# Spreading the adaLN modulation pairs of a two-block transformer kernel over more stages

## The reference

```python
def first_block(x, ...):
    ...
    h = rmsnorm(x, norm_ffn_pre[l])
    u = causal_depthwise_conv(h @ w_ffn_up[l], ffn_conv_w[l], ffn_conv_b[l])
    u_gate, u_val = jnp.split(u, 2, axis=-1)
    y = (jax.nn.gelu(u_gate, approximate=True) * u_val) @ w_ffn_down[l]
    return x + rmsnorm(y, norm_ffn_post[l])

def second_block(x, c, ctx, c_ctx, w_mod, b_mod, ...):
    for l in range(2):
        m_lat = (silu(c) @ w_mod[l] + b_mod[l]).reshape(9, 1024)
        m_ctx = (silu(c_ctx) @ w_mod[l] + b_mod[l]).reshape(9, 1024)
        x_lat = ffn_sublayer(x_lat, m_lat, 0, ...)      # rms_norm, scale and shift by m, swiglu, gate by m
        x_ctx = ffn_sublayer(x_ctx, m_ctx, 0, ...)
        p = modulate(rms_norm(x, ...), m, 1) @ w_in[l]   # q, k, v, fourier, gates
        ...                                              # attention, fourier mixing, gated merge
        x = ffn_sublayer(x, m, 2, ...)
```

## Time and profile before

| what | value |
|---|---|
| time, median of 3 runs | 2647.0 us (2645.97 to 2647.9) |
| profiled execution | 2647.9 us, its span 2646.1 us |
| TensorE busy | 2569.3 us, 97% of the span |
| VectorE busy | 1399.3 us, 53% |
| GpSimd busy | 1307.9 us, 49% |
| ScalarE busy | 1072.8 us, 41% |
| loaded from HBM | 363.19 MB, 138 GB/s over the span |

### The profile page before, as it was taken

How to read it: one execution, slowest core, us unless ns; L and a number is a source line. 1 busy time by engine, 2 the same in 40 slices (tenths; PEclk the granted TensorE clock), 3 DMA queues, 4 the chain that set the end, 5 groups by cost and what they waited for, 6 DMA issues and landing times.

```text
span 2646.1 us, 42582 instructions
## 1 busy us (share of the span) xinstructions
PE 2569.3 (97%) x14948; PEld 2232.8 (84%) x14948; DVE 1399.3 (53%) x3175; ACT 1072.8 (41%) x1934; POOL 1307.9 (49%) x654
## 2 busy tenths in 40 slices
PE   7999999999999999999999999999999999999998
PEld 7968999997788888877788888888888888889998
DVE  3656845358885420365476555665554443645221
ACT  4445457542223342266534222342222342565443
POOL 4515868754444443243344443444444453456885
PEclk8999989999999999999999999999999999999999
DMA  6714745635555432121234444544443452324563
GB/s 199 231 56 154 235 137 186 189 104 189 190 190 150 136 111 95 33 80 48 82 110 143 143 143 129 166 134 143 143 139 118 140 185 77 104 96 144 172 191 114
DMA packets 414006, 365.87 MB, mean 138 GB/s; under 512 B 7484, under 2 KB 412558, under 8 KB 413888
## 3 DMA queue, kind: packets, MB, share of 16 engines
q1 hardware_dynamic: 411448, 359.14, 43.0%
q10 hardware_dynamic: 2440, 5.16, 0.6%
HBM read 363.19 MB, written 1.08 MB: 138 GB/s over the span
## 4 chain that ended last, share of the span: by engine, by line
PE 74%; issue 11%; POOL 10%; DVE 3%; ACT 2%; DMA 0%; POOLq 0%; SPq 0%; ACTq 0%; DVEq 0%
PE bank L1978 61%; POOL w_lo L787 10%; PE bank L2498 2%; PE bank L2064 1%; PE bank L2538 1%; PE bank L2065 1%; PE bank L2069 1%; PE bank L2442 1%; PE bank L2310 1%; PE bank L2306 1%; DVE stat L1884 1%; ACT w_hi L837 1%; PE bank L2434 1%; PE bank L2190 1%; PE bank L2524 0%
## 5 line engine op out<-in xcount | busy, mean ns | idle before, releaser
L787 POOL TENSOR_TENSOR w_lo<-raw,w_hi 128x1024 fp32r<-128x1024 f32 (+3 forms) x558 | 1212.1, 2186 | 1153.1 <-ACT w_hi L837 1152.7
L837 ACT ACTIVATE w_hi<-raw 128x1024 fp32r<-128x1024 f32 (+3 forms) x558 | 533.0, 975 | 1014.4 <-PE bank L1978 703.8
L1978 PE MATMUL bank<-u_hi,w_hi 128*128 128x512 f32 (+1 forms) x2456 | 835.2, 340 | 8.3 <-POOL w_lo L787 4.0
L1978 PE MATMUL bank<-u_hi,w_lo 128*128 128x512 f32 (+1 forms) x2456 | 829.0, 338 | 0.0
L1978 PE MATMUL bank<-u_lo,w_hi 128*128 128x512 f32 (+1 forms) x2456 | 828.9, 338 | 0.0
L1978 PEld LDWEIGHTS bank<-u_hi,w_hi 128*128 128x128 f32 x2456 | 467.2, 190 | 81.9 <-issue 29.5
L1978 PEld LDWEIGHTS bank<-u_hi,w_lo 128*128 128x128 f32 x2456 | 467.4, 190 | 49.4
L1978 PEld LDWEIGHTS bank<-u_lo,w_hi 128*128 128x128 f32 x2456 | 467.6, 190 | 47.5
L1493 DVE SCALAR_TENSOR_TENSOR bank<-mod_raw,cond,bank 128x256 f32<-128x256 f32 x1008 | 401.4, 485 | 0.1
L1978 PE MATMUL bank<-hid_hi,w_hi 128*128 128x512 f32 (+1 forms) x880 | 305.6, 347 | 0.1
L1978 PE MATMUL bank<-hid_hi,w_lo 128*128 128x512 f32 (+1 forms) x880 | 305.0, 347 | 0.0
(11 more groups left out here) (272 smaller groups left out, 3424.2 us busy)
## 6 DMA issues: line engine op xcount, KB each, us to landing
raw<-in_ffn_w_in SPq DMA_DIRECT2D x88, 1024.0 KB, 5.1
mod_raw<-in_w_mod SPq DMA_DIRECT2D x144, 512.0 KB, 4.5
raw<-in_w_in SPq DMA_DIRECT2D x67, 1024.0 KB, 5.1
raw<-in_ffn_w_out SPq DMA_DIRECT2D x56, 704.0 KB, 4.7
raw<-in_w_ffn_up SPq DMA_DIRECT2D x22, 1024.0 KB, 5.1
raw<-in_w_attn_out SPq DMA_DIRECT2D x8, 1024.0 KB, 5.2
raw<-in_w_o SPq DMA_DIRECT2D x8, 1024.0 KB, 5.2
raw<-in_w_ffn_down SPq DMA_DIRECT2D x8, 704.0 KB, 4.6
```

The lines of the kernel that those rows point to most:

```text
L787: pool.tensor_tensor(st.half(t, w_lo[slot]), st.half(t, block), st.half(t, w_hi[slot]).bitcast(f32), ALU.subtract).then_inc(lo_ready, 1)
L837: act.activation(st.half(t, w_hi[(st.first + c) % 2]), st.half(t, raw_of(st, n)), ACT.Copy).then_inc(hi_ready, 1)
L1978: ins = pe.matmul(dst, s, v, start=first and n == 0, stop=final and n == 2)
```

## The change

Ten of the twenty pairs that `up_00` did are taken out of it (`mod=2` becomes `mod=1` over its bodies 1 to 10). They go to: `down1` (bodies 0, 1 and 2, one each), `down_00` (seven where there were four), `q_0` (one, in its second body), `k_0` (two) and `f_0` (one). The total, 36 for layer 0, stays. In `down1` DVE does the pair after the two tiles of the body, not between them. On ACT the context rows beside the last body of `down1` are grouped by block: four before the splits of (3,2) and four before those of (3,3), where they were taken two at a time before each half block.

```diff
-    gemm("down1", down(a["w_ffn_down"][0]), 16, per=4, kt=DOWN_KT, cols=P, banks=(0, 1), acc=2, ring=4)
+    gemm("down1", down(a["w_ffn_down"][0]), 16, per=4, kt=DOWN_KT, cols=P, banks=(0, 1), mod=1,
+         mod_bodies=range(3), acc=2, ring=4)
...
-        gemm(f"up_{l}0", pairs(a["ffn_w_in_2"][l, 0]), 22, mod=1 if last else 2, mod_bodies=range(1, 11), banks=(0, 1), **first)
+        gemm(f"up_{l}0", pairs(a["ffn_w_in_2"][l, 0]), 22, mod=1, mod_bodies=range(1, 11), banks=(0, 1), **first)
...
-             mod=1, acc=2, whole=True, shift=(f"n1_{l}", halves))
+             mod=1 if last else 2, acc=2, whole=True, shift=(f"n1_{l}", halves))
...
-        gemm(f"q_{l}", cols(w, 0), 4, **first)
-        gemm(f"k_{l}", cols(w, 1024), 4, mod=1 if last else 0)
+        gemm(f"q_{l}", cols(w, 0), 4, mod=0 if last else 1, mod_bodies=range(1, 2), **first)
+        gemm(f"k_{l}", cols(w, 1024), 4, mod=1)
         gemm(f"f_{l}", cols(w, 3072), 2, gpb=halves, banks=(0, 2) if last else (0, 1, 2, 3),
-             mod=1 if last else 0, token_major=True)
+             mod=1, token_major=True)
...
-                elif st.mod == 2:
+                elif st.mod == 2 or st.name == "down1":
...
                     for c in range(st.per):
+                        if final and beside is not None:
+                            beside(c)
                         for t in range(2):
-                            if final and beside is not None:
-                                beside(c, t)
...
-            def context_rows(c, t):
+            def context_rows(c):
 
-                for k in range(4 * c + 2 * t, 4 * c + 2 * t + 2 if c < 2 else 0):
+                for k in range(4 * c, 4 * c + 4 if c < 2 else 0):
...
                     for t in range(st.acc):
-                        if st.per == 4:
+                        if st.per == 4 and name != "down1":
                             for pair, step in pairs[t:t + 1]:
                                 mod_pair(st, pair, step)
...
+                    if name == "down1":
+                        for pair, step in pairs:
+                            mod_pair(st, pair, step)
```

## The result

The changed kernel takes 2658.6 us (median of 5 executions, 2655.8 to 2661.4); the kernel before took 2646.0 us beside it. The ratio is 1.0051, 95% interval 1.0037 to 1.0066. It is 12.6 us slower. I had said 2652.6 us (+5.6) and a range up to 2658.0, so the direction of the sum held and its size did not.

What follows compares the result with a forecast made beforehand. TensorE, busy 97% of the span, was taken as the bound. Terms -5.6 + 0 + 1.0 + 7.7 + 2.5 = +5.6 us on the profiled 2647.9 us, which lay 0.9 us above the median, gave 2652.6 us; 8-in-10 range 2647.5 to 2658.

Steps and rivals of the forecast that it cites:

- Part 3: down1: pair loads held in SP's queue make block (2,0) late, +1.0 us (+0.3 to +1.5), not adding up over bodies.
- Part 1: up_00: one pair less in each of ten bodies ends PE's loss, -5.6 us (-3.3 to -5.6).
- Part 2: down_00, q_0, k_0, f_0: the pairs moved there fit into DVE's free time and cost 0.
- Part 4: End of body 2 of down1: the third pair delays the context rows, so PE waits for (3,2), +7.7 us.
- Part 5: After the long PE wait in down1 the granted clock falls to 0.50 for a while, +2.5 us (1.7 to 3.4).
- Rivals A: down1: the pairs hide there too and DVE's late context rows cost nothing, sum -4.6, 2642.4 us; chance 0.12.
- B: down1's wait comes but the clock stays up, or up_00 gives more: 2650.1 us or down to 2649.4; chance 0.22.
- Rival C: down1: SP held behind mod_loads makes (2,0) and (3,0) late by 3 us each, sum +10.6, 2657.6 us; chance 0.13.
- Rival D: down1: DVE holds up POOL's operations, so three pairs cost 1.3 us more, 2653.9 us; chance 0.03.

Runs made afterwards that it cites:

- the second profile: The changed kernel run once more with no edit: 2659.0 us against 2645.6 for the kernel before (ratio 1.0050).
- Late loads with all three pairs: Changed kernel, with SP issuing the loads of down1's second and third pair later in its queue: 2651.8 us against 2645.6 for the kernel before (ratio 1.0023).

## Why the prediction was right or wrong

The forecast was +5.6 us and +12.6 us was measured. Four of the five parts held. Part 3 was too small by 3.1 us; with its measured size the sum would have been +8.7 us. Of the other 3.9 us, 0.3 us are part 1, and no run places the remaining 3.6 us.

**Part 1, `up_00`: right.** -5.3 us measured, -5.6 forecast. With one pair in each body PE is never idle there.

**Part 2, the other stages: right.** 237.2 us from the end of `up_00` to `v_0` against 237.3. DVE does its 7.8 us under a full PE.

**Part 4, the third pair in front of the context rows: right,** in mechanism and size. PE waited 7.59 us, forecast 7.7; ACT stood for DVE with the splits behind it. The 2 us of room that the grouping of the rows was to use up are there as well: without it PE waited 5.55 us. Taking the pair away brought body 3 back to 16.1 us.

**Part 5, the clock: right.** 2.6 us after this wait, forecast 2.5. Body 3 is 26.2 - 15.9 = 10.3 us longer, against 7.7 + 2.5 = 10.2. Rivals A (no wait) and B (no fall of the clock) go with these two parts.

**Part 3, the loads of the pairs: this is the step that failed.** I had +1.0 us, "between +0.3 and +1.5", and "It does not add up over bodies". It is 4.1 us, more than even my upper case of 3 us. The mechanism was the forecast one, but it was mis-sized at three places. First, (2,0) was to be ready 0.3 to 1.5 us late and was 2.3 us late in this profile (1.5 to 2.95 us in the seven profiles of kernels with these loads). SP issued it 0.3 us later than I had taken, and it took 6.4 us to land (512.50 to 518.87), where my bound was 5.8 (in the second profile it took 5.7). I had counted the chunk in front of it, but not the loads behind it: (2,1) was issued 0.6 us after (2,0) and (2,2) 2.3 us after, where before the next load had come 3.9 us later. This is SP's timeline:

```profile
508.48 3.47 SPq L728 DMA_DIRECT2D mod_raw<-in_w_mod  x2
512.50 2.08 SPq L715 DMA_DIRECT2D raw<-in_w_ffn_down  x2
514.84 5.11 SPq L715 DMA_DIRECT2D down_more<-in_w_ffn_down  x2
```

Second, after a wait of 2.3 us the clock fell as well, which cost 1.7 us; so it did in five of the seven profiles. I had priced the clock only for the long wait. The trace of before could have told me. The low clock of the earlier trace rows from 572 us on, which I took for the lower bound of part 5, came after two waits of PE of 0.55 and 1.61 us within 3 us:

```profile
572.97 0.47 PE L1978 MATMUL bank<-u_hi,w_hi 128*128 128x256 f32 x1 [1.61 <-DVE u_lo L1428]
```

Third, it can add up. Where the clock did not fall and all three pairs were there (the second profile), the lateness went on by a way that I had not followed: late load, ACT's splits, ACT's square behind them, DVE's sum, the next pair, the next load. Either way it came to 4 us.

**Rival C,** SP held behind the loads of the pairs: its mechanism is the one that the runs show, at 4 us for its 6 and beside the third pair, not larger than it. Late loads with all three pairs show that the bytes alone were no obstacle. Its 2657.6 us is nearer to the measured time than my forecast, but in part by luck, as it holds 2 us too much for the loads and none of the 3.6 us that nothing places.

**Rival D,** POOL held up by DVE: no. Beside the first pair of `down1` the 768-wide low part of the changed kernel took 1855 ns (first line); before, with no pair in the stage, the same took 1852 ns (second line). A 640-wide one that ran beside the two L1490 operations (504.46 to 506.03 us) took 1.57 us (third line), and their mean before was 1.57 us too. The rule, in the Trainium skill, page SBUF - State Buffer, section "Who interferes with whom", says that an operation of DVE with at most one SBUF input and outside the two-port modes does not contend with GpSimd, and these rows agree.

```profile
L788 POOL TENSOR_TENSOR w_lo<-down_more,w_hi 128x768 fp32r<-128x768 f32 x2 | 3.7, 1855 | 1.2 <-ACT w_hi L838 1.2
...
L787 POOL TENSOR_TENSOR w_lo<-down_more,w_hi 128x768 fp32r<-128x768 f32 x5 | 9.3, 1852 | 2.5 <-ACT w_hi L837 2.3
...
504.46 1.57 POOL L788 TENSOR_TENSOR w_lo<-raw,w_hi 128x640 fp32r<-128x640 f32 x1
```

**What the sum left out.** The stages explain 9.0 us (8.9 to 10.5 over four profiles of the changed kernel); the medians differ by 12.6 and 13.4 us, with an interval from 9.5 to 17.5. For the other kernels the stages against the medians are -2.7 and -1.8, +4.9 and +6.2, -5.2 and -3.7 (again -5.3 and -1.3), +7.8 and +8.8, -1.6 and +1.6, +15.7 and +14.6. The medians of before moved by 1.1 us. So 3 to 4 us of the changed kernel's loss are not placed. The parts outside these stages were 2094 to 2103 us long in the profiles; their mean is 2097.9 us over the four of the changed kernel and 2098.7 us over the eight others, so the profiles show no cost there, but their scatter is as large as what is open. The medians lie above the stages in all but one of these comparisons, and all use the one profile of before, whose execution was 1.9 us above its own median. A cost of some 2 us that all kernels with moved pairs share is therefore neither shown nor excluded.

## What to carry to other kernels

Free time of an engine is not a free place in its queue: `down1` had a DVE that was 88% idle, and one pair of 7.8 us at the wrong place cost 10 us, at another 3 to 4 us and in another stage nothing. Before work is moved to an idle engine, list what that engine does next and which other queue stands still for it; and list the loads of the moved work too, for an in-order queue that waits for the consumer's progress holds back every load behind it. A delay of a body should be followed once round the whole loop before it is called constant.

## What was not expected of the hardware

The clock fell after a wait of only 2.3 us in a PE that had been full on both sides (0.86 and 0.72 of the full clock in two stretches of 4 us), but not each time. At the start of body 2 it fell in the five profiles in which PE waited 2.3 to 2.95 us, and stayed at 1.00 in the two with 1.49 and 1.65 us, and after 1.66 us at the start of body 3. A short wait can thus cost nearly double its length. And a weight load of 704 KB, issued 0.9 us behind 512 KB for another buffer and with another 704 KB issued 0.6 us behind it, took 6.4 us to land, and 5.7 us in a second profile; the median of such loads before was 4.6 us. What the load in front and the ones behind each add is not shown.
